# The value products of sparse attention with the values stationary, in two column halves of TensorE

## The reference, cut to what matters

```python
s_cmp = einsum('bshgd,bchd->bhgsc', qg, kc) * scale
p_cmp = masked_softmax(s_cmp, mask_cmp)
o_cmp = einsum('bhgsc,bchd->bshgd', p_cmp, vc)
...
o_slc = lax.map(selected_block, (q_chunks, sel_chunks, pos_chunks))
...
o_win = einsum('bnhgqk,bnkhd->bnqhgd', p_win, vb).reshape(B, S, H, G, dh)
g = gates.reshape(B, S, H, G, 3)
o = g[..., 0:1] * o_cmp + g[..., 1:2] * o_slc + g[..., 2:3] * o_win
...
y_a = o_a @ w_nsa_branch[layer]
```

## Time and profile before

| | us |
|---|---|
| three runs | 1244.55, 1244.05, 1244.17 |
| median | 1244.17 |
| profiled execution, first to last instruction (span) | 1242.9 |
| TensorE busy in it | 1239.0 |
| VectorE / ScalarE / GpSimd busy | 957.8 / 722.1 / 422.0 |
| sparse attention, compressed scores to last value product | 77.2 to 165.8 |

### The profile page before, as it was taken

How to read it: one execution, slowest core, us unless ns; L and a number is a source line. 1 busy time by engine, 2 the same in 40 slices (tenths; PEclk the granted TensorE clock), 3 DMA queues, 4 the chain that set the end, 5 groups by cost and what they waited for, 6 DMA issues and landing times.

```text
span 1242.9 us, 17085 instructions
## 1 busy us (share of the span) xinstructions
PE 1239.0 (100%) x6634; PEld 1061.2 (85%) x6634; DVE 957.8 (77%) x1377; ACT 722.1 (58%) x1023; POOL 422.0 (34%) x338
## 2 busy tenths in 40 slices
PE   9999999999999999999999999999999999999999
PEld 8988788888888889888888888888988888888887
DVE  6875667677887478986878888986898597888895
ACT  7755545376765365577836555546457674655552
POOL 0010012039892069377420112008746750012100
PEclk9999999999999999999999999999999999999999
DMA  9753334555555448644554554465855454555442
GB/s 360 274 195 136 136 119 169 173 199 187 197 179 201 170 170 267 214 155 176 175 210 175 183 190 162 176 220 185 289 180 193 154 174 165 203 183 190 162 166 114
DMA packets 39008, 233.75 MB, mean 188 GB/s; under 512 B 4752, under 2 KB 5392, under 8 KB 13072
## 3 DMA queue, kind: packets, MB, share of 16 engines
q1 hardware_dynamic: 38928, 232.67, 53.4%
HBM read 225.31 MB, written 1.05 MB: 182 GB/s over the span
## 4 chain that ended last, share of the span: by engine, by line
PE 100%; DVE 0%; issue 0%; POOL 0%; POOLq 0%
PE ps L657 19%; PE ps L564 18%; PE ps L566 18%; PE ps L565 18%; PE ps L662 10%; PE ps L569 6%; PE ps L583 2%; PE ps L625 1%; PE ps L624 1%; PE ps L623 1%; PE ps L725 1%; PE ps L1209 1%; PE ps L700 0%; PE ps L893 0%; PE ps L810 0%; PE ps L811 0%
## 5 line engine op out<-in xcount | busy, mean ns | idle before, releaser
L1299 ACT ACTIVATE whi<-raw 128x2048 fp32r<-128x2048 f32 (+1 forms) x212 | 400.2, 1891 | 115.0 <-PE ps L566 101.5
L2052 DVE TENSOR_TENSOR wlo<-raw,whi 128x2048 fp32r<-128x2048 f32 x168 | 388.0, 2315 | 90.0 <-ACT whi L1299 89.3
L1885 POOL TENSOR_TENSOR wlo<-raw,whi 128x512 fp32r<-128x512 f32 x176 | 229.1, 1337 | 88.6 <-ACT whi L1299 85.6
L657 PE MATMUL ps<-hh,whi 128*128 128x512 f32 x1056 | 255.8, 391 | 0.0
L657 PEld LDWEIGHTS ps<-hh,whi 128*128 128x128 f32 x1056 | 193.0, 188 | 36.5
L564 PE MATMUL ps<-whi,hh 128*128 128x512 f32 (+1 forms) x504 | 201.3, 399 | 0.0
L566 PE MATMUL ps<-whi,hh 128*128 128x512 f32 (+1 forms) x504 | 195.5, 388 | 0.0
L565 PE MATMUL ps<-wlo,hh 128*128 128x512 f32 (+1 forms) x504 | 195.1, 387 | 0.0
L1857 POOL TENSOR_TENSOR st<-st,sm 128x1 f32<-128x1 f32 (+2 forms) x28 | 45.2, 1614 | 391.5 <-DVE st L2106 228.0
L662 PEld LDWEIGHTS ps<-hh,wlo 128*128 128x128 f32 x1056 | 137.8, 191 | 6.7
L662 PE MATMUL ps<-hh,wlo 128*128 128x256 f32 x1056 | 139.8, 282 | 0.0
(11 more groups left out here) (348 smaller groups left out, 2061.6 us busy)
## 6 DMA issues: line engine op xcount, KB each, us to landing
raw<-in_w SPq DMA_DIRECT2D x202, 1024.0 KB, 4.9
raw<-in_w SPq DMA_DIRECT2D x12, 256.0 KB, 6.7
gain<-in_bias SPq DMA_DIRECT2D x12, 256.0 KB, 5.0
kst<-kh SPq DMA_DIRECT2D x16, 128.0 KB, 2.8
qst<-qh SPq DMA_DIRECT2D x16, 128.0 KB, 2.3
raw<-in_w SPq DMA_DIRECT2D x2, 560.0 KB, 10.8
x<-in_x SPq DMA_DIRECT2D x4, 256.0 KB, 5.7
gain<-in_rows SPq DMA_DIRECT2D x2, 512.0 KB, 5.6
```

The lines of the kernel that those rows point to most:

```text
L657: pe.op.matmul(o[:, :], wh[:, k, c], t.hh[:, k, :, :], start=k == 0, stop=False, skip_group_check=True)
L1299: act.op.activation(t.whi[i % NHI][:, c], t.raw[i % NRAW][:, c], ACT.Copy).then_inc(*at("act_hi", ("hi", i)))
L1885: pool.op.tensor_tensor(t.wlo[i % NRAW][:, half(k)], t.raw[i % NRAW][:, half(k)], t.whi[i % NHI][:, half(k)].bitcast(F32), ALU.subtract).t ...
L2052: dve.op.tensor_tensor(t.wlo[i % NRAW][:, c], t.raw[i % NRAW][:, c], t.whi[i % NHI][:, c].bitcast(F32), ALU.subtract).then_inc(*at("dve_lo ...
```

## The change

The heads are taken in pairs, one of each key group. A unit's exponentials are multiplied by gate over sum in place, by GpSimd, before they are turned, so that all three branches can be summed in one PSUM bank. The values are stationary (64 columns) and the turned probabilities moving (128 columns): the head of group 0 fills partitions 0 to 63 of the result and the head of group 1 partitions 64 to 127, so the result is already turned. The exponentials are turned three steps behind their scores in place of two; `Ex` has four tiles and `ET` three. The compressed branch is normalized in `cp` ahead of its product. `oa`, `Tm` and the transposes of `oa` go; ScalarE copies the bank of token half 0 out to `o0`. `w_nsa_branch` is packed in the new order of heads.

```diff
-    return (2, int(place < 13))[tt]
+    return (2 if place < 12 else 1, int(place < 14))[tt]
+    units = [(tt, 4 * gr + j) for tt in range(2) for j in range(4) for gr in range(2)]
 TensorE
     def compressed(tt):
...
         if tt:
-            pe.wait_ge(*on("Tm", 7))
-        product(t.ob[:, :], t.cpT[:, :], t.VC[:, :, :], names=[("o cmp", tt)])
+            pe.wait_ge(*on("o0 out"))
+        for j in range(4):
+            product(t.ob[:, j * 128:j * 128 + 128], t.VC[:, 2 * j:2 * j + 2, :].rearrange("p a d -> p (a d)"), t.cpT[:, :],
+                    j == 0, False)
     def probs_turned(u):
-        pe.wait_ge(*on("exp", u))
+        pe.wait_ge(*on("Ex scaled", u))
     def values(u):
-        pe.wait_ge(*on("ET", u))
-        if u % 4 == 0:
-            pe.wait_ge(*on("oa cmp", tt) if u % 8 == 0 else on("Tm", u - 1))
+        for v in (u - 1, u):
+            pe.wait_ge(*on("ET", v))
         for a in range(2):
             for k in range(nk):
-                product(t.ob[:, ((hd % 4) * 2 + a) * 64:((hd % 4) * 2 + a) * 64 + 64], t.ET[u % 2][:, a * nk + k, :],
-                        t.qkv[k][:, 896 + 256 * a + 64 * gr:896 + 256 * a + 64 * gr + 64], k == 0, k == nk - 1,
+                for gr in range(2):
+                    last = a == 1 and k == nk - 1
+                    product(t.ob[64 * gr:64 * gr + 64, j * 128:j * 128 + 128],
+                            t.qkv[k][:, 896 + 256 * a + 64 * gr:896 + 256 * a + 64 * gr + 64],
+                            t.ET[(u - 1 + gr) % 3][:, a * nk + k, :], False, last, [("pv", u)] * (last and gr))
     def nsa():
-            for s in range(8 * tt, 8 * tt + 11):
-                if 8 * tt <= s - 2 < 8 * tt + 8:
-                    probs_turned(s - 2)
-                if 8 * tt <= s - 3:
-                    values(s - 3)
+            for s in range(8 * tt, 8 * tt + 12):
+                if 8 * tt <= s - 3 < 8 * tt + 8:
+                    probs_turned(s - 3)
+                if 8 * tt <= s - 4 and s % 2:
+                    values(s - 4)
     def retention():
-                heads_turned("oaT", t.oa, 4, lambda tt: ("oa", tt))
+                if k == 1:
+                    pe.wait_ge(*on("o lo", 1))
 ScalarE
     exps: waits for ("ExT", u - 4), was u - 3; probs_out at even s of unit s - 3
+            if tt == 0:
+                act.wait_ge(*on("pv", 7))
+                act.op.activation(t.o0[:, :, :], t.ob[...], ACT.Copy)
+    def o_upper():
+        act.wait_ge(*on("pv", 15))
+        act.op.activation(t.oah[:, :, tok(1)], t.ob[...], ACT.Copy)
+        act.wait_ge(*on("o0 out"))
+        act.op.activation(t.oah[:, :, tok(0)], t.o0[:, :, :], ACT.Copy)
 GpSimd
+    for u in range(16):
+        tt, hd = u // 8, u % 2 * 4 + u % 8 // 2
+        e = t.Ex[u % 4][:, :, 0:128 * (tt + 1)]
+        pool.wait_ge(*on("factor", u))
+        pool.op.tensor_tensor(e, e, bc(wq[:, tt, hd, :], [128, 2, 128 * (tt + 1)], 2), ALU.mult)
 VectorE
     def compressed(tt):
+        dve.op.tensor_tensor(t.cs[:, :, :], t.cs[:, :, :], bc(m01, [128, 8, 15], 1), ALU.mult)
+        await_own()
-        dve.op.tensor_tensor(t.cp[...], t.cs[:, :, :], bc(m01, [128, 8, 15], 1), ALU.mult)
+        dve.op.tensor_tensor(t.cp[...], t.cs[:, :, :], bc(r, [128, 8, 15], 2), ALU.mult)
...
-        dve.wait_ge(*on("o cmp", tt))
-        dve.op.tensor_tensor(t.oa[tt][...], t.ob[...], bc(r, [128, 8, 64], 2), ALU.mult)
-    def values(u):      (reciprocal, product with the gates, Tm, two additions to oa; every fourth unit)
+    def factor(u):
+        dve.wait_ge(*on("exp", u))
+        dve.op.reciprocal(f, lw[:, tt, hd, :])
+        await_own()
+        dve.op.tensor_tensor(f, f, gates[:, tt, hd, 1:3], ALU.mult)
     def nsa():
+                if 8 * tt <= s - 3 < 8 * tt + 8 and s % 2:
+                    probs_out(s - 3)
+                if 8 * tt <= s - 1 < 8 * tt + 8:
+                    factor(s - 1)
                 if s < 8 * tt + 8:
                     score_max(s)
+    for tt, src in ((1, t.ob[...]), (0, t.o0[:, :, :])):
+        lower([("o lo", tt)], t.oal[:, :, tok(tt)], src, t.oah[:, :, tok(tt)], ("o hi", tt))
```

More of the change, by code:

```diff
@@ L340, in place @@
     t.k1h, t.k1l = (at(n, n0 + a, [128, 2, 2, S], R32) for n, a in (("k1h", 10.5), ("k1l", 30.5)))
[L341 to L344, removed]
+    t.Ex = [at(f"Ex{i}", n0 + (16.5, 18.5, 14.5, 26.5)[i], [128, 2, S]) for i in range(4)]
+    t.ET = [at(f"ET{i}", n0 + 20.5 + 2 * i, [128, 4, 128]) for i in range(3)]
+    t.o0 = at("o0", n0 + 28.5, [128, 4, 128])
     t.Sw = at("Sw", n0 + 30.5, [128, 2, 16, 32])
@@ L846, in pe_program @@
     run(g)
-    units = [(tt, hd) for tt in range(2) for hd in range(8)]
+    units = [(tt, 4 * gr + j) for tt in range(2) for j in range(4) for gr in range(2)]
     def compressed(tt):
@@ L893, in probs_turned @@
                 ins = pe.op.transpose(t.tp[:, (a * nk + k) * 128:(a * nk + k) * 128 + 128],
-                                      t.Ex[u % 3][:, a, k * 128:k * 128 + 128], ident)
+                                      t.Ex[u % 4][:, a, k * 128:k * 128 + 128], ident)
         ins.then_inc(*at("pe_turned", ("ExT", u)))
@@ L898, in values @@
         tt, hd = units[u]
-        gr, nk = hd // 4, tt + 1
-        pe.wait_ge(*on("ET", u))
-        if u % 4 == 0:
-            pe.wait_ge(*on("oa cmp", tt) if u % 8 == 0 else on("Tm", u - 1))
+        j, nk = hd % 4, tt + 1
+        for v in (u - 1, u):
+            pe.wait_ge(*on("ET", v))
         for a in range(2):
             for k in range(nk):
-                product(t.ob[:, ((hd % 4) * 2 + a) * 64:((hd % 4) * 2 + a) * 64 + 64], t.ET[u % 2][:, a * nk + k, :],
-                        t.qkv[k][:, 896 + 256 * a + 64 * gr:896 + 256 * a + 64 * gr + 64], k == 0, k == nk - 1,
-                        [("pv", u)] * (a == 1 and k == nk - 1))
+                for gr in range(2):
[3 more added lines that the diff above has]
+                            t.ET[(u - 1 + gr) % 3][:, a * nk + k, :], False, last, [("pv", u)] * (last and gr))
     def nsa():
@@ L958, in retention @@
             yield 2
-            if hd == 0:
-                heads_turned("oaT", t.oa, 4, lambda tt: ("oa", tt))
             yield 1
@@ L971, in pe_program @@
     for tt in range(2):
-        pe.wait_ge(*on("free", ("oaT", tt, 0)))
+        pe.wait_ge(*on("o lo", tt))
     short_rows("ya0", t.oah, t.oal)
@@ L1494, in exps @@
         act.wait_ge(*on("max", u))
-        if u >= 3:
-            act.wait_ge(*on("ExT", u - 3))
+        if u >= 4:
+            act.wait_ge(*on("ExT", u - 4))
         for a in range(2):
-            act.op.activation(t.Ex[u % 3][:, a, 0:n], s[:, a, 0:n], ACT.Exp, bias=nm[:, tt, hd, a:a + 1],
+            act.op.activation(t.Ex[u % 4][:, a, 0:n], s[:, a, 0:n], ACT.Exp, bias=nm[:, tt, hd, a:a + 1],
                               accum_out=lw[:, tt, hd, a:a + 1]).then_inc(*at("act_out", *([("exp", u)] * a)))
@@ L1503, in probs_out @@
         act.wait_ge(*on("ExT", u))
-        if u >= 2:
-            act.wait_ge(*on("pv", u - 2))
-        act.op.activation(t.ET[u % 2][:, 0:n, :], t.tp[:, 0:n * 128].rearrange("p (k s) -> p k s", k=n),
+        if u >= 3:
+            act.wait_ge(*on("pv", (u - 3) | 1))
+        act.op.activation(t.ET[u % 3][:, 0:n, :], t.tp[:, 0:n * 128].rearrange("p (k s) -> p k s", k=n),
                           ACT.Copy).then_inc(*at("act_out", ("ET", u)))
@@ L1518, in nsa @@
                     ret_turned("kr", 0)
-            for s in range(8 * tt, 8 * tt + 11):
-                if 8 * tt <= s - 2 < 8 * tt + 8 and s % 2:
-                    probs_out(s - 2)
+            for s in range(8 * tt, 8 * tt + 12):
+                if 8 * tt <= s - 3 < 8 * tt + 8 and s % 2 == 0:
+                    probs_out(s - 3)
                 if s < 8 * tt + 8:
@@ L1527, in nsa @@
                     ret_turned("kr", 1)
+            if tt == 0:
+                act.wait_ge(*on("pv", 7))
+                act.op.activation(t.o0[:, :, :], t.ob[:, :].rearrange("p (k s) -> p k s", k=4), ACT.Copy).then_inc(
+                    *at("act_out", ("o0 out",)))
+    def o_upper():
+        act.wait_ge(*on("pv", 15))
+        act.op.activation(t.oah[:, :, tok(1)], t.ob[:, :].rearrange("p (k s) -> p k s", k=4), ACT.Copy).then_inc(
+            *at("act_small", ("o hi", 1)))
+        act.wait_ge(*on("o0 out"))
+        act.op.activation(t.oah[:, :, tok(0)], t.o0[:, :, :], ACT.Copy).then_inc(*at("act_small", ("o hi", 0)))
     def value_out(u, dst, after, scale=None):
@@ L1548, in act_program @@
     weave(nsa(), back)
-    heads_upper("oaT", 4, t.oah)
+    o_upper()
     def retention():
@@ L1901, in pool_program @@
             *at("pool_small", ("kr", "rot", tt)))
+    wq = st[:, 448:480].rearrange("p (t h a) -> p t h a", t=2, a=2)
+    for u in range(16):
+        tt, hd = u // 8, u % 2 * 4 + u % 8 // 2
+        e = t.Ex[u % 4][:, :, 0:128 * (tt + 1)]
+        pool.wait_ge(*on("factor", u))
+        pool.op.tensor_tensor(e, e, bc(wq[:, tt, hd, :], [128, 2, 128 * (tt + 1)], 2), ALU.mult).then_inc(
```

(24 more changed lines are left out.)

## The result

The changed kernel takes 1246.9 us (median of 12 runs, 1246.3 to 1247.5) against 1244.5 for the kernel before in the same comparison (12 runs, 1243.9 to 1245.0): a ratio of 1.0020, with a 95% interval from 1.0012 to 1.0028. It is slower by 2.4 us, at the edge of the 0.2% named ahead; 1240.7 was forecast, with a range from 1238.3 to 1243.8.

A forecast was written before the change was run, and what follows sets the result against it. TensorE's own list of work was taken to bound the kernel, provided its suppliers stay ahead. Value products -3.2, oaT transposes -0.87, cp +0.3 and stalls +0.3 gave -3.5 us from 1244.17: 1240.7 us, range 1238.3 to 1243.8.

The forecast's parts named there:

- Part 1: Value products on TensorE: column halves run at once, 10.8 us become 7.6 with edges, a gain of 3.2 us.
- the form used for the estimate: Line 765's matmuls in two partition halves: 32 take 1.09 us, with edges of 0.23 entering and 0.20 leaving.
- Rival A: Value products: the halves don't overlap at 128 columns, 12.7 us with edges in place of 10.8; 1245.8 us, chance 0.08.
- Part 2: Other TensorE work: the eight oaT transposes go, gain 0.87 us; the compressed product stays at 0.86 per token half.
- A stage far behind the attention that becomes longer: Sign of a wrong forecast: a later stage lengthens because a supplier was only just in time; no size given.
- Part 3: Compressed softmax: extra VectorE work ahead of cp exposes 0.3 us at token half 0, nothing at half 1.
- Part 4: VectorE, ScalarE, GpSimd in the attention: a 3.4 us path from scores to transposes, covered by the third step of delay.
- 0.3 us in for stalls: TensorE's allowance for late suppliers in the attention; its ends were 0 and the price of rival B.
- ScalarE's bias and weight splits are untouched: Statement on ScalarE's queue in the attention: the change leaves these splits alone; no cost was entered.
- the tie of factor and maximum: VectorE's maximum waits behind the previous unit's factor: a 2.2 us loop per unit, falling behind under 1 us, then recovering.
- rival B: Second token half: the VectorE-ScalarE loop becomes the bound, 8.3 us of stalls in place of 0.3; 1248.7 us, chance 0.08.
- rival C: Attention: rival B in part, a few late units, 1 to 3 us of stalls; 1241.4 to 1243.4 us, chance 0.18.

The follow-up runs named there:

- e1: Changed kernel with the ring of four PSUM banks turned on by two places where the oaT transposes took two banks; 1245.8 us, ratio 1.0011.
- e5: Kernel before with only the ring of PSUM banks turned on by two places behind its oaT transposes; 1245.4 us, ratio 1.0009.
- e7: Changed kernel with ring turned on, ET copies exchanged between VectorE and ScalarE in token half 0 alone, maximum ahead of factor; 1241.2 us, ratio 0.9976.
- e4: e3 with VectorE's maximum of unit s put ahead of the factor of unit s-1; 1241.3 us, ratio 0.9977.
- e12: Changed kernel with only VectorE's maximum put ahead of the factor, ring and copies as changed; 1244.1 us, ratio 0.9998.
- e3: Changed kernel with ring of PSUM banks turned on and ET copies exchanged between VectorE and ScalarE in both token halves; 1243.1 us, ratio 0.9991.
- e9: e3 without GpSimd's scaling of the exponentials, VectorE's factor kept in its place; 1243.0 us, ratio 0.9990.

## Why the prediction was wrong

**Part 1, the value products: right, 0.4 us too large.** The blocks of TensorE in the chain of after, token half 1 (160 to 164 us):

```profile
161.84 0.44 PE ps L894 x4
162.28 1.02 PE ps L568 x16
163.31 0.43 PE ps L563
163.74 0.24 PE ps L564
```

Sixteen matmuls of 128 columns take 1.02 us, 0.064 each: the column halves do run at once (one stream alone is 0.107). The 0.43 behind them in place of 0.23 is the edge, the same 0.20 as in the form used for the estimate. Together 1.22 for a block, where 1.16 was reckoned (16 x 0.054 and 0.30); a block of half 0 is 0.59 and 0.20 (0.73 reckoned). Four of each are 8.0 us against 10.8 before, a gain of 2.8 and not of 3.2. Rival A is out. The Trainium skill states that a change of the tiling mode drains the engine (TensorEngine Tiling (Array Packing), Key Properties). These 0.20 us agree with it.

**Part 2: right on its face, wrong in what hangs on it.** The transposes of oaT went, 0.87 us. The step "the eight transposes go: gain 0.87" failed in that these transposes also took two turns of the ring of banks. Removing them cost 1.0 us elsewhere (e1, e5), more than they took. A stage far behind the attention that becomes longer stood among the signs of being wrong, but it had no price.

**Part 3: right for token half 0, 0.2 us short for half 1.** cp delays TensorE by 0.3 us at token half 0 (0.55 from start to start in place of 0.23) in every run of the changed form. At half 1 the text has "nothing"; in after and e7 its transpose comes 0.2 us late (0.42 in place of 0.23). A weight split of 2.29 us stands ahead of VectorE's chain there (in after at 129.51, with the compressed scores at 129.41), so that the chain begins 2.3 us behind the scores.

**Part 4: wrong, and this is the step that decided.** The text asked whether the path of one unit, from scores through GpSimd to the transposes, fits into three steps, and it does: no wait for GpSimd in the changed kernel. It put 0.3 us in for stalls, against 4.2 measured in five pauses. What it did not do is to follow the copy of ET, which the same step of delay moved: it stands ahead of maximum and factor in VectorE's queue, and behind the background split of the step before. "ScalarE's bias and weight splits are untouched" was true of the splits and missed that something else had moved behind them. In the tie of factor and maximum the place was named, as rival B, but only for the second half and as a bound on throughput. It worked as a delay, most in the first half, where one pair of steps holds a split on each of the two engines in series (1.81, then 2.29 us). And of this tie the text says that VectorE "falls behind by under 1 us and recovers"; taking it out gave 1.8 us in e4 and 2.7 in e12.

Rival B's mechanism took part, then, at another place and with another price: 4.2 us in place of 8.3, and more than the 1 to 3 us of rival C. B with 0.08 and C with 0.18 were too little for it.

The sum has two slips that decide nothing. Without edges and without stalls it gives 1238.0 us (5.6 + 0.87 - 0.3 = 6.2 under 1244.2), not 1238.3 or the 1239 of "its own range"; and rival B's two steps of 2.4 and two of 3.4 are 11.6, not 11.7.

**The account.** Value products -2.8, oaT -0.87, cp +0.3 and +0.2: -3.2. e7 measures -3.1 in the stretch of the attention and -3.0 in the median. TensorE's matmuls are the same in after and in e7, so their starts can be compared one by one: in the attention after is 4.5 us longer (129.4 against 124.9), 4.2 of it in the five pauses and the rest in smaller ones, and at the up product 1.0. -3.1 + 4.5 + 1.0 = +2.4, as measured.

## What to carry to other kernels

When a step is moved by one in a schedule where engines take turns by odd and even, everything that it issues changes its neighbours: list for each queue what now stands right ahead of it, the moved copies first and not only the new operation, and ask of a long operation ahead whether it waits for another engine. A removed user of a rotating resource (a bank, a buffer) shifts all that come after it; compare the order in which such a resource is handed out before and after, or put the turns back. And where a new small operation waits for another engine, put it behind the operation that others wait for.

## What the runs showed of the hardware

The shared access of GpSimd and VectorE works in both directions. In the changed kernel VectorE's weight split, 2.29 us otherwise, took 2.75 when it started inside a scaling on GpSimd; and a scaling that started inside a split took 3.03 in place of 1.04 us. VectorE, then GpSimd:

```profile
149.71 2.75 DVE L2074 TENSOR_TENSOR wlo<-raw,whi 128x2048 fp32r<-128x2048 f32 x1
```

```profile
149.26 1.04 POOL L1922 TENSOR_TENSOR Ex<-Ex,st 128x512 f32<-128x512 f32 x1 [1.67 <-DVE st L2400]
```

```profile
160.88 3.03 POOL L1922 TENSOR_TENSOR Ex<-Ex,st 128x512 f32<-128x512 f32 x1 [1.95 <-DVE st L2400]
```

The split's 0.46 us of delay is close to the 0.59 for which the scaling still ran (149.26 + 1.04 - 149.71). The Trainium skill says so (SBUF — State Buffer, SBUF: two separate sides): whichever comes first holds the pair for its whole instruction. The trace agrees both ways. The slower scaling held nobody up: TensorE waits for no scaled exponentials in after. The slower split is a piece of after's chain of waits (149.79, 2.67), ahead of the pause of 0.56 us at 156.2; what its 0.46 us cost there no run shows. In e3, which has such a split as well, they cost nothing (e9). A 128x512 product with a broadcast factor takes GpSimd 1.04 us alone, one of 128x256 0.61.
